# Moving one first projection in four of a dense expert layer from the expert stage into the routing-map stage, and a subtraction from VectorE to GpSimd

## Chip, cores and metric

One core of one Trainium2 chip. The metric is the device time of one execution in microseconds, the median of several. The kernel is one launch of several stages, which are parted by barriers over all engines.

## What is computed

The reference is one step of a decoder layer: attention, then a retrieval layer (PEER) in which each of 1056 tokens picks 128 of 16384 experts. Only that second half matters here:

```
q = (tb @ wq) ...; s = q . keys; top-16 of 128 first keys and of 128 second keys, top-16 of their sums
e = i1 * 128 + i2                      # expert number, weight g = softmax of the scores
a = gelu(einsum('td,thkd->thk', tb, u_tab[e]))
out = einsum('thk,thkd->td', g * a, v_tab[e])
```

The kernel computes 640 of the tokens (five tiles of 128) densely: for every first key (128 of them, each with 128 experts) it takes the projections of all 640 tokens on the key's `u` rows, gelu, times a map G of weights that is zero almost everywhere, and multiplies by the key's `v` rows. The other 416 tokens are done by gathers of single expert rows. Products are made in three parts of split numbers: high by high, high by low, low by high.

## The kernel before

**Map stage** (second part of `peer_route`, lines 1488 to 2021). For each of five tiles (ND) it goes through 32 groups (NGT) of 4 tokens, 160 groups in all. For each token TensorE multiplies two one-hot matrices of 128x128 (L2013), which makes that token's map. Of each group three left one-hots come from GpSimd (L1946), three right ones from VectorE (`rows`, L1660), and the fourth pair from ScalarE (`make`, L1881 to L1888). ScalarE moves the result out of PSUM (`leave`, L1898), and SP stores it to scratch in ten transfers of 4 MB (L1643). One-hots and maps have four slots (SLOTS), so that no engine is more than four groups ahead of TensorE. VectorE does the searches of the other tiles in between, in an order written out (`between`).

**Expert stage** (`peer_experts`, lines 2032 to 2396). It has 32 turns (NQ), each of four first keys (CQ). A turn has two halves. In the **dots half** there are eight slots m (two for each key, one for each block of 320 tokens). TensorE makes 24 products of 128x320 for each slot (L2168, L2169, L2174) into one of two PSUM banks; ScalarE takes the gelu (L2226); VectorE multiplies by the map (`weigh`, L2329); ScalarE copies the high part `ph` (L2232); VectorE subtracts it for the low part `pl` (L2334). In the **out half** TensorE makes 16 sums of 12 products each (L2190: high v by high p, L2195: low v by high p, L2199: high v by low p), and VectorE adds each to the accumulator (L2343).

The rounded parts of u and v are made by ScalarE (`split_u` L2214, `split_v` L2220) and GpSimd (`low_u` L2359, `low_v` L2363). The 416 gathered rows of a partition run beside all this, 13 in a turn: GpSimd issues the gather (L2368), VectorE takes a dot product (L2297) and later the weighted sum (L2309), with two small ScalarE operations between. The tuple BESIDE says how many dots or sums go with which slot: (2, 2, 2, 1, 2, 1, 1, 0) in the dots half, then none and 15 times one. The ring of gathered rows has four places. In the dots half GpSimd goes through the slots in order: in slots 1 and 3 `low_u`, in slots V_AT = (0, 2, 4, 5) `low_v`, then the slot's gathers. In each slot every engine's order is fixed by the program; semaphores count slots. The third sum of out slot 0 waits until the `pl` of slot 6 is there, and the second until all four `low_v` are.

Of the kernel before, what the change touches and what calls it, by code (L numbers as in the profile page):

```python
# [1489 lines left out]
def peer_route(nc, io, keep):  # L1490
# [32 lines left out]
    with ExitStack() as ctx:  # L1523
# [87 lines left out]

        with nc.Block() as block:
            @block.sync
            def _(sp):
# [25 lines left out]
                def store(i):  # L1640
                    for h in range(2):
                        sp.wait_ge(g_out, NGT * i + GROUPS * (h + 1))
                        sp.dma_start(gview[2 * i + h], G[:, h].rearrange("p i t -> p (i t)")).then_inc(g_stored[h], 16)  # L1643

                load(0)
                for i in range(ND):
                    if i + 1 < LATE:
                        load(i + 1)
                    store(i)

            @block.vector
            def _(v):
# [149 lines left out]
                def turn(i):  # L1802
                    v.wait_ge(pick_turned, i + 1)
                    if i >= 2:
                        v.wait_ge(spread, NGT * (i - 1))
                    pickT = pickTs[:, i % 2]
                    turned = turned_at(i)
                    nc.vector.tensor_copy(pickT[:, 0:3], turned[:, 0:3 * P].rearrange("p (n t) -> p n t", n=3))
                    nc.vector.tensor_scalar(pickT[:, 3], turned[:, 2 * P:3 * P], -1.0, None, ALU.mult).then_inc(pick_out, 1)
                    v.wait_ge(pick_out, i + 1)  # L1810

# [7 lines left out]
                def between():  # L1819

                    spots[0] += 1
                    for n in range(made[0], rows_before(spots[0])):
                        if n % NGT == 0:
                            turn(n // NGT)
                        rows(n // NGT, n % NGT)
                    made[0] = rows_before(spots[0])
# [7 lines left out]
            def _(act):  # L1834
# [55 lines left out]

                def leave(i, g):
# [11 lines left out]
                for i in range(ND):  # L1903
                    for g in range(NGT):
                        for n in range(LATE):
# [6 lines left out]
                        if i < ND - 1 and g % COPY_EVERY == 0:  # L1912
                            copy_window(act, io, "k", PER_TILE * i + g // COPY_EVERY).then_inc(keep.win_out, 16)
                    if NGT * (i + 1) == spread_at:
# [6 lines left out]
            def _(pool):  # L1921
# [8 lines left out]

                for i in range(ND):
                    pickT = pickTs[:, i % 2]
                    pool.wait_ge(pick_out, i + 1)
                    for q in range(NGT // SLOTS):
# [7 lines left out]
                        for u in range(SLOTS):  # L1942
                            if done + u >= SLOTS:
# [12 lines left out]
            def _(pe):  # L1956
# [35 lines left out]

                pe.wait_ge(keys_in, 16)
# [8 lines left out]
                for i in range(ND):  # L2002
                    for g in range(NGT):
# [10 lines left out]
                        x.then_inc(spread, 1)  # L2014

# [10 lines left out]
DOTS = CQ * NBD  # L2026
OUTS = NBD * KC
# [4 lines left out]
def peer_experts(nc, io, keep):  # L2032


    with ExitStack() as ctx:
# [18 lines left out]
        Gt = G.rearrange("p u h (c t) -> p u h c t", c=2)  # L2054
        hrow = sb("e_hrow", [P, D])[:]
# [11 lines left out]
        uv_in = [nc.alloc_semaphore(f"e_uv_in{u}") for u in range(RING)]  # L2067
        h_in = nc.alloc_semaphore("e_h_in")
# [21 lines left out]
        V_AT = (0, 2, 4, 5)  # L2090
# [31 lines left out]
        with nc.Block() as block:  # L2122
            @block.sync
            def _(sp):
# [7 lines left out]
                def load_u(i, c):  # L2132

                    sp.wait_ge(ul_done, CQ * i + c - 1)
                    sp.dma_start(uu[:, c % 2], uview[ds(CQ * i + c, 1)].rearrange("a p k e -> (a p) k e")).then_inc(u_in[c % 2], 16)
# [11 lines left out]
                for c in (2, 3):  # L2147
                    load_u(0, c)
                with sp.Fori(0, NQ - 1) as i:
                    for load, c in ((load_v, 2), (load_u, 4), (load_v, 3), (load_g, 4), (load_u, 5), (load_v, 4), (load_v, 5),  # L2150
                                    (load_g, 6), (load_u, 6), (load_u, 7)):
                        load(i, c)
# [4 lines left out]
            def _(pe):  # L2157
# [3 lines left out]
                def dot(i, c):  # L2161
                    pe.wait_ge(uh_done, CQ * i + c + 1)
                    for b in range(NBD):
                        m = NBD * c + b
                        pe.wait_ge(p_done, DOTS * i + m + 1)
                        cols = slice(b * WD, (b + 1) * WD)
                        for k in range(KC):
                            nc.tensor.matmul(pa[:, m % 2, 0:WD], uh[:, c % 2, k], keep.hi_d[:, k, cols], start=(k == 0), stop=False)  # L2168
                            nc.tensor.matmul(pa[:, m % 2, 0:WD], uh[:, c % 2, k], keep.lo_d[:, k, cols], start=False, stop=False)  # L2169

                        if b == 0:
                            pe.wait_ge(ul_done, CQ * i + c + 1)
                        for k in range(KC):
                            x = nc.tensor.matmul(pa[:, m % 2, 0:WD], ul[:, c % 2, k], keep.hi_d[:, k, cols], start=False,  # L2174
# [28 lines left out]
                with pe.Fori(0, NQ) as i:  # L2203
                    for c in range(CQ):
                        dot(i, c)
                    out(i)

            @block.scalar
            def _(act):
# [12 lines left out]
                def gelus(i, m):  # L2222
                    n = DOTS * i + m
                    c, b = m // NBD, m % NBD
                    act.wait_ge(dotted, n + 1)
                    nc.scalar.activation(pa[:, m % 2, 0:WD], pa[:, m % 2, 0:WD], ACT.Gelu).then_inc(gelu_done, 1)  # L2226
                    if b == 1 and c < 2:
                        split_u(CQ * i + 2 + c)
# [39 lines left out]
                act.dma_start(uu[:, 0], uview[0]).then_inc(u_in[0], 16)  # L2268
                act.dma_start(uu[:, 1], uview[1]).then_inc(u_in[1], 16)
# [6 lines left out]
                for i in range(NQ):  # L2276
# [5 lines left out]
                    for n in range(OUTS):  # L2282
                        if n in (0, 2) and i + 1 < NQ:
                            split_u(CQ * (i + 1) + n // 2)
# [4 lines left out]
            def _(v):  # L2289
# [32 lines left out]
                def weigh(i, m):  # L2322
# [3 lines left out]
                    ops = share(m)  # L2326
# [3 lines left out]
                                            pa[:, m % 2, 0:WD].rearrange("p (h t) -> p h t", h=ND),  # L2330
# [308 lines left out]
```

## Time and profile before

| what | value |
|---|---|
| median of 3 runs | 3917.97 us (3907.5 to 3925.23) |
| the profiled execution | 3920.84 us, span 3919.2 us |
| TensorE busy | 3292.2 us (84%) |
| VectorE busy | 2633.8 us (67%) |
| GpSimd busy | 1600.8 us (41%) |
| ScalarE busy | 1347.6 us (34%) |
| query part of the routing stage | about 1225 to 1545 us |
| map stage | 1545 to 1898 us |
| expert stage | 1913 to 3838 us |

Busy times are unions over an engine's instructions. The records of TensorE products overlap, so the pace of products is read from the starts of two of them, not from the duration of one. An average over the span mixes stages with different limits, so each stage is read by itself.

### The profile page before, as it was taken

What the parts mean: (1) busy time and instruction counts of PE and PEld (TensorE: products, weight loads), DVE (VectorE), ACT (ScalarE), POOL (GpSimd) and SP (SyncE); (2) the same over time, 40 slices, a digit from 0 to 9 for tenths busy, and PEclk for the clock granted to TensorE, in tenths of its full rate; (3) what the DMA queues carried; (4) which work ended last, traced back from release to release, by engine and by line L of the source; (5) the groups of instructions that cost most, each with busy time, mean ns of one, the idle gap of its engine ahead of it and who ended that gap; (6) DMA issues with size and microseconds to landing.
All of it is one profiled execution on the core that took longest, in us unless ns stands there. A gap on an engine that the chain in (4) does not pass through costs nothing. (4 is left out here: it accounts for less than half of the span.)

```text
span 3919.2 us, 58752 instructions
## 1 busy us (share of the span) xinstructions
PE 3292.2 (84%) x20585; PEld 2874.9 (73%) x20585; DVE 2633.8 (67%) x5881; ACT 1347.6 (34%) x3190; POOL 1600.8 (41%) x1345
## 2 busy tenths in 40 slices
PE   6999688656587975666699999999999999999994
PEld 3778455211277964555599999999999999999993
DVE  3224676101133799999588888888888888888885
ACT  3010466100222113878433333333333333333331
POOL 1010000000121444999645555545546455455450
PEclk8999899877788987878799999999999999999997
DMA  6631783799512222664688889888888898888883
GB/s 221 240 131 65 216 227 130 309 412 411 210 61 97 65 69 69 250 244 197 265 316 339 313 316 342 315 325 334 307 329 326 313 340 314 320 326 315 312 295 132
DMA packets 280225, 991.40 MB, mean 253 GB/s; under 512 B 21781, under 2 KB 139392, under 8 KB 215721
## 3 DMA queue, kind: packets, MB, share of 16 engines
q1 hardware_dynamic: 214504, 480.69, 33.9%
q0 software_dynamic: 62784, 469.88, 31.7%
q10 hardware_dynamic: 2752, 38.75, 2.6%
q8 instruction: 70, 1.15, 0.1%
q14 instruction: 115, 0.93, 0.1%
HBM read 909.51 MB, written 146.80 MB: 270 GB/s over the span
## 5 line engine op out<-in xcount | busy, mean ns | idle before, releaser
L2168 PE MATMUL e_pa<-k_hi_d,e_uh 128*128 128x320 f32 x2048 | 618.2, 315 | 76.3 <-DVE e_act L2329 60.6
L2169 PE MATMUL e_pa<-k_lo_d,e_uh 128*128 128x320 f32 x2048 | 607.9, 311 | 0.0
L2368 POOL DMA_INDIRECT e_uv<-peer_uv,k_g_idx x416 | 399.9, 961 | 498.9 <-DVE e_pY L2309 443.4
L2297 DVE CUSTOM_DVE_ANT_0 e_uv<-e_uv,e_h 128x1024 f32<-128x1024 f32 x416 | 503.7, 1211 | 62.4 <-DMA e_uv<-peer_uv,k_g_idx 62.2
L2309 DVE SCALAR_TENSOR_TENSOR e_pY<-e_uv,e_wts,e_pY 128x1024 f32<-128x1024 f32 x412 | 526.9, 1279 | 0.0
L2168 PEld LDWEIGHTS e_pa<-k_hi_d,e_uh 128*128 128x128 f32 x2048 | 387.3, 189 | 101.6 <-DVE e_act L2329 85.7
L2363 POOL TENSOR_TENSOR e_vl<-e_v,e_vh 128x1024 fp32r<-128x1024 f32 x128 | 308.8, 2413 | 292.8 <-ACT e_vh L2220 292.2
L2247 ACT ACTIVATE e_gel<-e_dots 128x1 f32<-128x1 f32 x416 | 83.5, 201 | 957.1 <-DVE e_dots L2297 956.8
L2190 PE MATMUL e_po<-e_ph,e_vh 128*128 128x320 f32 x2048 | 387.0, 310 | 15.3 <-DVE k_OT L2343 11.0
L2169 PEld LDWEIGHTS e_pa<-k_lo_d,e_uh 128*128 128x128 f32 x2048 | 387.5, 189 | 0.0
L2199 PE MATMUL e_po<-e_pl,e_vh 128*128 128x320 f32 x2048 | 384.0, 309 | 0.4
L2195 PE MATMUL e_po<-e_ph,e_vl 128*128 128x320 f32 x2048 | 383.4, 309 | 0.0
L2013 PE MATMUL r_pG<-k_OT 128*128 128x128 f32 x1280 | 224.8, 336 | 157.4 <-issue 53.0
L2359 POOL TENSOR_TENSOR e_ul<-e_u,e_uh 128x1024 fp32r<-128x1024 f32 x128 | 309.0, 2414 | 116.2 <-ACT e_uh L2214 114.9
L2174 PE MATMUL e_pa<-k_hi_d,e_ul 128*128 128x320 f32 x2048 | 342.5, 309 | 0.0
L2190 PEld LDWEIGHTS e_po<-e_ph,e_vh 128*128 128x128 f32 x2048 | 320.4, 188 | 22.9 <-DVE k_OT L2343 17.5
L2013 PEld LDWEIGHTS r_pG<-k_OT 128*128 128x128 f32 x1280 | 199.9, 239 | 182.4 <-issue 119.0
L1946 POOL TENSOR_SCALAR k_OT<-k_iota,r_second 128x128 f32<-128x128 f32 x480 | 325.7, 698 | 8.5 <-PE r_pG L2013 4.7
L2199 PEld LDWEIGHTS e_po<-e_pl,e_vh 128*128 128x128 f32 x2048 | 321.2, 188 | 1.4 <-DVE e_pl L2334 1.4
L2195 PEld LDWEIGHTS e_po<-e_ph,e_vl 128*128 128x128 f32 x2048 | 321.3, 188 | 0.0
L2174 PEld LDWEIGHTS e_pa<-k_hi_d,e_ul 128*128 128x128 f32 x2048 | 311.6, 188 | 0.0
L2334 DVE TENSOR_TENSOR e_pl<-e_act,e_ph 128x320 fp32r<-128x320 f32 x256 | 273.7, 1069 | 17.2 <-ACT e_ph L2232 14.5
(326 smaller groups left out, 5919.7 us busy)
## 6 DMA issues: line engine op xcount, KB each, us to landing
k_kv<-kv_pages SPq DMA_DIRECT2D x128, 512.0 KB, 6.2
s_kv<-kv_state SPq DMA_DIRECT2D x32, 2048.0 KB, 17.5
e_v<-peer_uv SPq DMA_DIRECT2D x128, 512.0 KB
e_u<-peer_ut SPq DMA_DIRECT2D x126, 512.0 KB
s_g<-r_G SPq DMA_DIRECT2D x10, 4096.0 KB
k_OT<-s_g SPq DMA_DIRECT2D x64, 640.0 KB
v_win_sample<-state_v_win POOLq DMA_DIRECT2D x28, 1168.0 KB
k_win_sample<-state_k_win ACTq DMA_DIRECT2D x28, 1168.0 KB
```

Source lines behind the costliest of these rows:

```text
L1946: x = nc.gpsimd.tensor_scalar(hot2[:, u, t], keep.iota[:], second[:, u, t:t + 1], None, ALU.is_equal)
L2013: x = nc.tensor.matmul(pG[:, u, t], hot2[:, u, t], hot1[:, u, t], start=True, stop=True)
L2168: nc.tensor.matmul(pa[:, m % 2, 0:WD], uh[:, c % 2, k], keep.hi_d[:, k, cols], start=(k == 0), stop=False)
L2169: nc.tensor.matmul(pa[:, m % 2, 0:WD], uh[:, c % 2, k], keep.lo_d[:, k, cols], start=False, stop=False)
L2174: x = nc.tensor.matmul(pa[:, m % 2, 0:WD], ul[:, c % 2, k], keep.hi_d[:, k, cols], start=False, stop=(k == KC - 1))
L2190: nc.tensor.matmul(po[:, n % SUMS, 0:WD], vh[:, c, rows], ph[:, c, cols], start=(c == 0), stop=False)
L2195: nc.tensor.matmul(po[:, n % SUMS, 0:WD], vl[:, c, rows], ph[:, c, cols], start=False, stop=False)
L2199: x = nc.tensor.matmul(po[:, n % SUMS, 0:WD], vh[:, c, rows], pl[:, c, cols], start=False, stop=(c == CQ - 1))
L2297: nc.vector.tensor_tensor_reduce(uv[:, r, 0:D], uv[:, r, 0:D], h[:], 1.0, 0.0, ALU.mult, ALU.add, dots[:, r:r + 1]).then_inc(row_dotted, 1)
L2309: x = nc.vector.scalar_tensor_tensor(out=pY[:], in0=uv[:, r, D:2 * D], scalar=wts[:, r:r + 1], in1=pY[:], op0=ALU.mult, op1=ALU.add)
L2359: nc.gpsimd.tensor_tensor(ul[:, c % 2], uu[:, c % 2], uh[:, c % 2], ALU.subtract).then_inc(ul_done, 1)
L2368: nc.gpsimd.indirect_dma_start(uv[:, s % RING], None, io["peer_uv"], bass.IndirectOffsetOnAxis(ap=keep.g_idx[:, s:s + 1], axis=0),).then_i ...
```

## The change

The first projections of the first of each turn's four keys (32 keys, 64 halves of 24 products, 1536 products) are made in the map stage. There TensorE makes some 10 of them after each group from group 12 on (`made_by`). The u rows are loaded by SP, split by ScalarE and GpSimd, the result is copied out of PSUM by ScalarE and stored by SP to a new scratch `s_p`. In the expert stage slots 0 and 1 of a turn have no products: their projections are loaded from scratch, and gelu and map product work in SBUF. Three keys in place of four are loaded and split in a turn. The low part `pl` goes from VectorE to GpSimd, before the slot's gathers, and VectorE's `weigh` waits until the `pl` of two slots before is done. `low_v` goes with slots (1, 2, 4, 5), the only `low_u` of the dots half with slot 3.

```diff
 # map stage
+        def made_by(done):
+            return max(0, HALVES * PER_HALF * (done + 1 - OPENS) // (ND * NGT - OPENS))
+        def half_at(n):
+            return next(g for g in range(ND * NGT) if made_by(g) >= PER_HALF * (n + 1))
 # SP
+                def load_u(e):
+                    if e >= 2:
+                        sp.wait_ge(ul_done, e - 1)
+                    sp.dma_start(uu[:, e % 2], io["peer_ut"][CQ * e]).then_inc(u_in[e % 2], 16)
+                def store_p(e):
+                    sp.wait_ge(p_out, NBD * e + NBD)
+                    sp.dma_start(io["s_p"][e], pout[:, e % 2]).then_inc(p_stored[e % 2], 16)
...
+                store_p(EARLY - 1)
+                for u in range(2):
+                    sp.wait_ge(p_stored[u], 16 * (EARLY // 2))
 # ScalarE
+                    nc.scalar.activation(uh[:, e % 2], uu[:, e % 2], ACT.Copy).then_inc(uh_done, 1)
...
+                    nc.scalar.activation(pout[:, e % 2, b * WD:(b + 1) * WD], pa[:, n % 2, 0:WD], ACT.Copy).then_inc(p_out, 1)
 # GpSimd
+                def low_u(e):
+                    pool.wait_ge(uh_done, e + 1)
+                    nc.gpsimd.tensor_tensor(ul[:, e % 2], uu[:, e % 2], uh[:, e % 2], ALU.subtract).then_inc(ul_done, 1)
...
+                            for e in range(2, EARLY):
+                                if done + u == half_at(NBD * (e - 2) + 1) + SLOTS:
+                                    low_u(e)
 # TensorE
                         x.then_inc(spread, 1)
+                        for m in range(made_by(done - 1), made_by(done)):
+                            early_dot(m)
 # expert stage
-        V_AT = (0, 2, 4, 5)
+        V_AT = (1, 2, 4, 5)
 # SP
+                def load_early(i):
+                    sp.wait_ge(p_done, DOTS * i + NBD + 2)
+                    sp.dma_start(early, io["s_p"][ds(i + 1, 1)].rearrange("a p t -> (a p) t")).then_inc(early_in, 16)
 # TensorE
-                    for c in range(CQ):
-                        dot(i, c)
-                    out(i)
+                        for c in range(1, CQ):
+                            dot(2 * j + half, half, c)
+                        out(2 * j + half)
 # VectorE
-                    ops = share(m)
+                    own = early[:, b * WD:(b + 1) * WD] if c == 0 else pa[:, m % 2, 0:WD]
+                    if n >= 2:
+                        v.wait_ge(pl_done, n - 1)
                     v.wait_ge(g_in[c // 2], 16 * i + 16)
                     v.wait_ge(gelu_done, n + 1)
...
-                    gathers(i, ops[:1])
-                    v.wait_ge(ph_done, n + 1)
-                    nc.vector.tensor_tensor(pl[:, c, cols], act_out[:, m % 2], ph[:, c, cols], ALU.subtract).then_inc(pl_done, 1)
-                    gathers(i, ops[1:])
+                    gathers(i, share(m))
 # GpSimd
+                def low_p(i, m):
+                    n, c, b = DOTS * i + m, m // NBD, m % NBD
+                    cols = slice(b * WD, (b + 1) * WD)
+                    pool.wait_ge(ph_done, n + 1)
+                    nc.gpsimd.tensor_tensor(pl[:, c, cols], act_out[:, m % 2], ph[:, c, cols], ALU.subtract).then_inc(pl_done, 1)
...
-                        if m % NBD == 1 and m // NBD < 2:
-                            low_u(CQ * i + 2 + m // NBD)
+                        if m == 3:
+                            low_u(UQ * i + 2)
                         if m in V_AT:
                             low_v(CQ * i + V_AT.index(m))
+                        low_p(i, m)
                         gathers(i, m)
```

## Rows read from the trace of the kernel before

**Rows 1.** Busy time by stretch (stretch, length; engine busy, instructions; granted clock, DMA share, GB/s).
```profile
1371.00:1545.00 174.00, 106.91 (x546) 99.28 (x544) 168.89 (x537) 25.26 (x65) 67.55 (x34) 0.82 0.21 61
1545.00:1900.00 355.00, 225.84 (x1289) 200.93 (x1289) 326.00 (x1342) 300.55 (x799) 338.77 (x521) 0.80 0.54 212
...
1960.00:3780.00 1820.00, 1752.37 (x11731) 1720.13 (x11730) 1507.67 (x2171) 620.11 (x1526) 964.38 (x640) 1.00 0.86 323
```
**Rows 2.** Groups of the map stage, 1545 to 1900 us (busy, mean ns | idle before, releaser).
```profile
L1946 POOL TENSOR_SCALAR k_OT<-k_iota,r_second 128x128 f32<-128x128 f32 x478 | 324.5, 698 | 8.4 <-PE r_pG L2013 4.7
L2013 PE MATMUL r_pG<-k_OT 128*128 128x128 f32 x1280 | 224.8, 336 | 157.4 <-issue 53.0 <-DVE k_OT L1660 48.2 <-POOL k_OT L1946 42.1
```
**Rows 3.** Groups of the expert stage, 1960 to 3780 us, same columns.
```profile
L2168 PE MATMUL e_pa<-k_hi_d,e_uh 128*128 128x320 f32 x1937 | 581.0, 314 | 52.0 <-DVE e_act L2329 52.0
...
L2297 DVE CUSTOM_DVE_ANT_0 e_uv<-e_uv,e_h 128x1024 f32<-128x1024 f32 x399 | 483.2, 1211 | 60.7 <-DMA e_uv<-peer_uv,k_g_idx 60.5
...
L2363 POOL TENSOR_TENSOR e_vl<-e_v,e_vh 128x1024 fp32r<-128x1024 f32 x121 | 292.0, 2413 | 280.5 <-ACT e_vh L2220 279.9
...
L2334 DVE TENSOR_TENSOR e_pl<-e_act,e_ph 128x320 fp32r<-128x320 f32 x241 | 256.6, 1065 | 16.2 <-ACT e_ph L2232 13.5 <-issue 2.7
...
L2214 ACT ACTIVATE e_uh<-e_u 128x1024 fp32r<-128x1024 f32 x121 | 126.0, 1041 | 0.0
```
**Rows 4.** GpSimd's groups over the whole span: subtractions of other widths.
```profile
L1929 POOL TENSOR_TENSOR q_wl<-r_G,q_wh 128x1024 fp32r<-128x1024 f32 x32 | 85.8, 2682 | 2.6
...
L1311 POOL TENSOR_TENSOR k_lo_d<-k_OT,k_hi_d 128x640 fp32r<-128x640 f32 x8 | 12.3, 1538 | 0.0
L1310 POOL TENSOR_TENSOR k_lo_g<-k_OT,k_hi_g 128x416 fp32r<-128x416 f32 x8 | 8.5, 1066 | 49.3 <-ACT k_hi_d L1238 49.3
```
**Rows 5.** Timeline of TensorE, one turn (start, length, operation).
```profile
3024.32 0.74 PE L2190 MATMUL e_po<-e_ph,e_vh 128*128 128x320 f32 x4
...
3053.33 0.31 PE L2168 MATMUL e_pa<-k_hi_d,e_uh 128*128 128x320 f32 x1
...
3056.85 0.31 PE L2168 MATMUL e_pa<-k_hi_d,e_uh 128*128 128x320 f32 x1
...
3083.97 0.74 PE L2190 MATMUL e_po<-e_ph,e_vh 128*128 128x320 f32 x4
```
**Rows 6.** Timeline of VectorE, then of GpSimd, start of a dots half.
```profile
3053.94 1.21 DVE L2297 CUSTOM_DVE_ANT_0 e_uv<-e_uv,e_h 128x1024 f32<-128x1024 f32 x1
...
3057.57 0.49 DVE L2329 TENSOR_TENSOR e_act<-e_pa,k_OT 128x320 f32<-128x320 f32 x1 [2.41 <-ACT e_pa L2226]
...
3059.17 0.48 DVE L2334 TENSOR_TENSOR e_pl<-e_act,e_ph 128x320 fp32r<-128x320 f32 x1
3059.57 1.21 DVE L2297 CUSTOM_DVE_ANT_0 e_uv<-e_uv,e_h 128x1024 f32<-128x1024 f32 x1
...
3061.78 0.49 DVE L2329 TENSOR_TENSOR e_act<-e_pa,k_OT 128x320 f32<-128x320 f32 x1 [0.99 <-ACT e_pa L2226]
...
3063.38 2.53 DVE L2334 TENSOR_TENSOR e_pl<-e_act,e_ph 128x320 fp32r<-128x320 f32 x1
...
3059.60 2.42 POOL L2363 TENSOR_TENSOR e_vl<-e_v,e_vh 128x1024 fp32r<-128x1024 f32 x1 [4.93 <-ACT e_vh L2220]
...
3065.71 1.03 POOL L2368 DMA_INDIRECT e_uv<-peer_uv,k_g_idx  x1 [0.16 <-issue]
```
**Rows 7.** Timeline around the end of the map stage.
```profile
1893.30 1.13 PE L2013 MATMUL r_pG<-k_OT 128*128 128x128 f32 x8 [0.39 <-issue]
...
1898.56 0.33 SPq L1643 DMA_DIRECT2D s_g<-r_G  x1
...
1911.48 1.85 SPq L2130 DMA_DIRECT2D k_OT<-s_g  x2
...
1913.58 0.63 PE L2168 MATMUL e_pa<-k_hi_d,e_uh 128*128 128x320 f32 x1 [15.68 <-ACT e_uh L2214]
```
**Rows 8.** The page's DMA issues (KB each, us to landing).
```profile
k_kv<-kv_pages SPq DMA_DIRECT2D x128, 512.0 KB, 6.2
```

More of the change, by code:

```diff
@@ L1810, in turn, with keep_turned @@
                     v.wait_ge(pick_out, i + 1)
+                def keep_turned():
+                    for i in range(2, ND):
+                        v.wait_ge(pick_turned, i + 1)
+                        nc.vector.tensor_copy(kept_turned[:, i - 2], turned_at(i)[:, 0:3 * P]).then_inc(turned_kept, 1)
                 for x in range(NHC):
@@ L1904, in _ @@
                     for g in range(NGT):
+                        if i == 0 and g in (SLOTS, SLOTS + 1):
+                            split_u(g - SLOTS)
+                        for n in range(HALVES):
+                            if NGT * i + g == half_at(n) + 1:
+                                dots_away(n)
+                                if n % NBD == NBD - 1 and n // NBD + 2 < EARLY:
+                                    split_u(n // NBD + 2)
                         for n in range(LATE):
@@ L1913, in _ @@
                             copy_window(act, io, "k", PER_TILE * i + g // COPY_EVERY).then_inc(keep.win_out, 16)
+                    if i == ND - 1:
+                        for n in range(HALVES):
+                            if half_at(n) == ND * NGT - 1:
+                                dots_away(n)
                     if NGT * (i + 1) == spread_at:
@@ L2026 @@
 DOTS = CQ * NBD
+UQ = CQ - 1
 OUTS = NBD * KC
@@ L2054, in peer_experts @@
         Gt = G.rearrange("p u h (c t) -> p u h c t", c=2)
+        early = keep.rest[:, 4 * DT:5 * DT]
         hrow = sb("e_hrow", [P, D])[:]
@@ L2145, in load_v, with quad @@
                     sp.dma_start(vv[:, c % 2], row(vview, CQ * i + c)).then_inc(v_in[c % 2], 16)
[L2147 to L2152, printed above, removed]
+                def load_early(i):
+                    sp.wait_ge(p_done, DOTS * i + NBD + 2)
+                    sp.dma_start(early, io["s_p"][ds(i + 1, 1)].rearrange("a p t -> (a p) t")).then_inc(early_in, 16)
+                def quad(i, half):
+                    load_u(i, half, UQ)
+                    load_v(i, 2)
+                    load_early(i)
+                    load_v(i, 3)
+                    load_u(i, half, UQ + 1)
+                    load_g(i, 4)
+                    load_v(i, 4)
+                    load_v(i, 5)
+                    load_g(i, 6)
+                    load_u(i, half, UQ + 2)
+                sp.dma_start(early, io["s_p"][0]).then_inc(early_in, 16)
+                load_u(0, 0, 2)
+                with sp.Fori(0, NQ // 2 - 1) as j:
+                    for half in range(2):
+                        quad(2 * j + half, half)
+                quad(NQ - 2, 0)
                 for c in (2, 3):
@@ L2201, in out @@
                             x.then_inc(summed, 1)
-                with pe.Fori(0, NQ) as i:
-                    for c in range(CQ):
-                        dot(i, c)
-                    out(i)
+                with pe.Fori(0, NQ // 2) as j:
+                    for half in range(2):
+                        for c in range(1, CQ):
+                            dot(2 * j + half, half, c)
+                        out(2 * j + half)
             @block.scalar
@@ L2224, in gelus @@
                     c, b = m // NBD, m % NBD
[L2225 to L2228, printed above, removed]
+                    if c == 0:
+                        own = early[:, b * WD:(b + 1) * WD]
+                        act.wait_ge(early_in, 16 * i + 16)
+                    else:
+                        own = pa[:, m % 2, 0:WD]
+                        act.wait_ge(dotted, NBD * UQ * i + m - NBD + 1)
+                    nc.scalar.activation(own, own, ACT.Gelu).then_inc(gelu_done, 1)
+                    if m == 3:
+                        split_u(UQ * i + 2)
                     act.wait_ge(p_done, n + 3)
@@ L2394, in _ @@
                         if n in (0, 2) and i + 1 < NQ:
-                            low_u(CQ * (i + 1) + n // 2)
+                            low_u(UQ * (i + 1) + n // 2)
                         gathers(i, DOTS + n)
```

118 lines of the change are left out of this document (94 added, 24 removed).

## The prediction

> **What bounds the kernel now.** I read the page, then busy time by stretch, then the groups and the timeline of the two stages that the change touches. In the expert stage TensorE is busy for 1752 of 1820 us at full granted clock, VectorE for 1508, GpSimd for only 964 [rows 1]: TensorE sets the pace. A turn has 64 products of L2168, of which 1937 fall into 1820 us, so a turn takes 1820 / (1937/64) = 60.1 us [rows 3]. One turn in detail [rows 5]: out half 3024.32 to 3053.33, 29.0 us; dots half 3053.33 to 3083.97, 30.6 us. A slot of 24 products takes 3.52 us, 0.1466 us for one. 192 products are 28.15 us, so the out half loses 0.85 us and the dots half 2.5 us to waits.
>
> In the map stage it is GpSimd: busy for 339 of 355 us, against 326 on VectorE, 301 on ScalarE and 226 on TensorE [rows 1], which stands idle for 157 us in its group [rows 2]. GpSimd's one-hots waited for TensorE only 4.7 us. So the change takes work from where TensorE is the bound to where it has room, but each moved key also brings a GpSimd subtraction to a stage that GpSimd bounds.
>
> **Map stage: GpSimd.** Added are 32 `low_u` of 128x1024. The same subtraction takes 2.413 us in the expert stage [rows 3]: 77 us. Beside VectorE's searches the like of it took 2.68 us [rows 4]: 86 us. Lower end 61 us, if all 16 idle us of GpSimd are filled. I take 77 plus 5 for waits behind VectorE's long operations: **+82 us**, a stage of 437 us.
>
> **Map stage: the other engines.** TensorE: eight 128x128 products take 1.13 us [rows 7], 0.141 each at most, so 1280 are at most 180 us; the 1536 moved ones at 0.1466 are 225 us. Sum 405 us at full clock, below 437. The clock was 0.80 there [rows 1], at a TensorE that was busy 64% of the time and slowed down whenever it waited; at 0.93 and more the 405 still fit, below that they don't (a rival). ScalarE gets 32 splits at 1.04 us [rows 3] and 64 copies of 320 columns, priced at 0.49 (VectorE's operation on as many, [rows 6]): 33 + 31, 365 of 437 us. VectorE gets three short copies, 2 us. All this is covered by GpSimd's 437 us; if GpSimd had more room, TensorE's 405 would be next. SP gets 32 loads and 32 stores between the ten map stores. A 4 MB store took 1898.56 to 1911.48, 12.9 us [rows 7], and a u load queued behind it waits as long; the program gives each load about five groups, 5 x 2.7 = 13 us. Cost taken as nothing; upper end in the rival.
>
> **Between the stages.** Now TensorE starts 15.0 us after the last map store is issued [rows 7]: the first u rows of the expert stage queue behind it. In the changed kernel SP must see the last `store_p` land before the barrier, and that store stands behind the map store: 12.9 us, then some 1.3 us of barrier, then a 512 KB load, whose nearest row is 6.2 us [rows 8], and a split of 1.04: 21.5 us. **+6.5 us** (0 to 10).
>
> **Expert stage: what TensorE saves.** 48 products in a turn, 48 x 0.1466 = 7.0 us, or 225 us in 32 turns, if TensorE keeps the pace. VectorE loses 241 subtractions of 257 us in this stretch, 8.5 us a turn [rows 3]; of its 49.8 (1508 / 30.3 turns) 41.3 us are left, with 2 us a turn of waits for gathered rows (60.5 us in L2297), so it bounds nothing. The question is GpSimd.
>
> **The price of the moved subtraction.** 416 columns took 1.066 us and 640 took 1.538 [rows 4], 2.11 ns per column, so 320 take **0.864 us** (bounds: 0.75 by proportion to 2.413 us for 1024, and 1.07). By the Trainium skill (GPSIMD Engine Reference, Elementwise, and Engine selection: use VectorE, GpSimd is about 2x slower with two inputs, some 2.6 cycles of 1.2 GHz per element) it would be an estimated 0.69 us with no fixed part; the chain below would be 1.0 us shorter and the forecast 33 us lower.
>
> **A turn walked through.** Let t = 0 at 3053.33, when TensorE starts the dots. VectorE's last dot product of the turn before starts at 3053.94 [rows 6]. From such a start to the next `weigh` it is 3061.78 - 3059.57 = 2.21 us (dot, two small ScalarE operations, gelu), so with its gelu input already there, `weigh` of slot 0 comes at 0.61 + 2.21 = 2.8 (now 4.2). Slots with two gather operations have a pitch of 3061.78 - 3057.57 = 4.21 now; less the 0.40 of the subtraction, 3.81. So `weigh` of slots 1 and 2 comes at 6.6 and 10.4. TensorE starts with slots 2 and 3 and has used both banks at 7.0; it waits for `weigh` 2 until 10.9.
>
> GpSimd: the first `low_v` is now in slot 1, behind that slot's `weigh`, `ph` and `split_v`; now it starts 3059.60 - 3057.57 = 2.03 us after the `weigh` [rows 6], so at 8.6. From there GpSimd never gets free until the `pl` of slot 6, on which the third sum of the out half waits. In program order: four `low_v` and one `low_u`, 5 x 2.41 = 12.1; the `pl` of slots 1 to 6, 6 x 0.864 = 5.2; the gathers of slots 1 to 4, each 0.15 + 1.03 [rows 6], 4.7; gaps 0.3. Sum 22.3, end at **30.9**. TensorE meanwhile: slot 4 from 10.9 to 14.4, slot 5 from the end of `weigh` 3 (10.4 + 3.8 + 0.5 = 14.7) to 18.2, slot 6 to 21.8, slot 7, which needs `weigh` 5 and by the new wait `pl` 3 (done at 21.0), to 25.3. It then makes 8 of the 192 out products and stands until 30.9; 184 are left: 184 x 0.1466 = 27.0, plus the 0.85 us that the out half loses today: the turn ends at **58.75**. Against 60.1 that is 1.4 us, **-44 us** in 32 turns instead of the 225. Bounds: with the `pl` at 0.75, 22 us more gain; with TensorE's pace reached, the rival below; with the first `low_v` or the v loads late by a microsecond or two, no gain, 0 us.
>
> What is queued behind GpSimd's new waits: its gathers. The gather of slot 4 goes out at about 25.6, where the ring needs the row some 9 us later; nothing more is lost there. The DMA moves 323 GB/s at a share of 0.86 [rows 1]; a turn loads a u of 0.52 MB less and 0.33 MB of projections more, so with 58.75 us it stays at about 327 GB/s.
>
> **Sum.** 3920.8 + 82 + 6.5 - 44 = 3965 for this execution, which lay 2.9 us over the median of the runs: **3962 us**, 1.1% slower. A measurement of this kernel tells a change of about 0.5% (20 us) from none.
>
> **Rivals.**
> - **TensorE keeps the pace of the expert stage** (faster). If the GpSimd chain ends before TensorE wants it, a turn is 336 x 0.1466 = 49.3 plus today's 3.4 of waits, 52.7: -237. With +88 outside it gives 3769. For it: GpSimd's work (7 x 2.41, 13 gathers at 1.03, 8 x 0.864) is 37 us in a turn of 52.7; VectorE loses its only operation that is held behind GpSimd (2.53 us against 0.48, [rows 6]). Against: of that work 22 us stand in one string that can't start before slot 1. Chance 0.12.
> - **The gain and the cost meet.** GpSimd's string ends some 2 us earlier (slots' `weigh` earlier, a cheaper `pl`), a turn of 56.5 to 57.5: -83 to -115. With +75 to +88 outside this gives 3875 to 3925, about 3905. Chance 0.23.
> - **The map stage stalls** (slower still). TensorE's 405 us at the clock of 0.80 would be 506 us; or u loads wait behind the ten map stores for 5 us each, and ScalarE with them. It decides once the granted clock stays under 405/437 = 0.93. The stage is then 460 to 505 us: 3985 to 4030. For it: the clock was 0.82 in the stretch before too, with TensorE busy 61% [rows 1]. Against: a TensorE that lags is busy all the time, and wherever it is, as in the expert stage, the clock is 1.00. By the Trainium skill (GPSIMD Engine Reference, Specifications) GpSimd shares its SBUF interfaces with VectorE's instructions that have two SBUF inputs; the 2.53 us row agrees, and this would add to this case. Chance 0.15.
> - **The forecast's own case**, 3930 to 3985, has 0.50.
>
> **Range and chances.** The range leaves out the first rival (0.12) and the outer part of the stalls: 3880 to 4015. Faster by over 0.5% (below 3898): the first rival and half of the second, 0.24. Within 0.5%: the rest of the second and the edge of the forecast, 0.17. Slower: 0.59.
>
> **What the profile would show.** Right: a map stage of 430 to 445 us with GpSimd busy throughout and TensorE idle in short pieces; in the expert stage a turn of 58 to 59 us, TensorE below 90% busy, L2199 waiting for GpSimd's `pl` by some 4 us a turn and L2168 for `weigh`; the GpSimd subtraction of 320 columns at 0.86 us. Wrong: a turn near 53 us; GpSimd idle in the dots half after slot 1; a map stage near 355 us, which would mean that GpSimd had room; or ScalarE waiting for u loads.

## The result, and the profile after

The changed kernel takes 4065.7 us (median of 4), the kernel before 3921.3 in the same runs: 1.036 times as long (95% interval 1.034 to 1.039). The forecast was 3962. Busy time by stretch of the changed kernel, columns as in [rows 1]; the map stage first, then the inside of the expert stage:

```profile
1547.00:2073.00 526.00, 402.35 (x2817) 394.32 (x2818) 364.22 (x1345) 355.94 (x893) 403.02 (x552) 0.88 0.53 192
...
2140.00:3920.00 1780.00, 1598.29 (x10255) 1569.45 (x10254) 1279.14 (x1925) 601.31 (x1494) 1081.94 (x849) 0.95 0.89 326
```

The map stage is 171 us longer than before (355 in [rows 1]), and in it no engine is busy for more than 403 of 526 us. That is what a stage looks like whose engines wait in turn for something outside them. Its groups:

```profile
L2036 POOL TENSOR_SCALAR k_OT<-k_iota,r_second 128x128 f32<-128x128 f32 x477 | 313.7, 676 | 2.9
L2127 PE MATMUL r_pG<-k_OT 128*128 128x128 f32 x1280 | 185.9, 292 | 151.9 <-issue 106.4 <-POOL k_OT L2036 34.1 <-DVE k_OT L1708 11.4
...
L2014 POOL TENSOR_TENSOR q_wl<-r_u,q_wh 128x1024 fp32r<-128x1024 f32 x32 | 78.3, 2448 | 113.8 <-ACT q_wh L1952 113.4
...
L1952 ACT ACTIVATE q_wh<-r_u 128x1024 fp32r<-128x1024 f32 x32 | 33.6, 1050 | 106.7 <-DMA r_u<-peer_ut 106.7
```

L1952 is `split_u` of the map stage: ScalarE stood still for 106.7 us until u rows were loaded, GpSimd's `low_u` (L2014) 113 us for ScalarE. Here is one of these waits, SP's issues and then ScalarE's split in the timeline:

```profile
1700.73 0.33 SPq L1668 DMA_DIRECT2D s_g<-r_G  x1
1701.10 0.43 SPq L1673 DMA_DIRECT2D r_u<-peer_ut  x1
1701.58 0.92 SPq L1677 DMA_DIRECT2D s_p<-r_pout  x1
1702.54 1.24 SPq L1648 DMA_DIRECT2D k_OT<-s_s  x1
1703.83 1.26 SPq L1673 DMA_DIRECT2D r_u<-peer_ut  x1
...
1721.06 1.06 ACT L1952 ACTIVATE q_wh<-r_u 128x1024 fp32r<-128x1024 f32 x1 [16.27 <-DMA r_u<-peer_ut]
```

The 4 MB map store goes out first, the u load 0.4 us behind it, and its rows are there 20 us later; ScalarE has waited 16.3 us, so it wanted them 3.7 us after they were asked for. While it waits it neither takes maps out of PSUM nor makes its one-hots, and with four slots all engines stop. Nine such waits fall in the stage, about one for each map store. Over the nine, ScalarE wanted the rows 3.7 to 13.9 us after the issue of the load (9 on average), and they landed 13.7 to 25.5 us after it (21 on average).

The store itself is longer than the one in [rows 7]. By the packet records of the trace its last packet ends 18.7 us after its issue, not 12.9. The DMA queues of these microseconds (1700.8 to 1719.4; packets, MB, share of the 16 engines) show what runs beside it: q1 is SP's queue, q10 ScalarE's, on which a copy of 1168 KB (`k_win_sample`) is under way:

```profile
q1 hardware_dynamic: 392, 5.29, 77.8%
q10 hardware_dynamic: 39, 1.20, 17.6%
```

It was so in the kernel before too: eight of its ten map stores take 17.7 to 24.6 us, with 1.2 MB or more moved on ScalarE's queue meanwhile, and only the last two, with 0 and 0.4 MB, take 10.8 and 12.3. [rows 7] shows the last of all. The ninth store of the changed kernel has nothing beside it, and the load behind it lands 13.7 us after its issue:

```profile
2024.96 0.33 SPq L1668 DMA_DIRECT2D s_g<-r_G  x1
2025.34 0.43 SPq L1673 DMA_DIRECT2D r_u<-peer_ut  x1
...
2039.09 1.06 ACT L1952 ACTIVATE q_wh<-r_u 128x1024 fp32r<-128x1024 f32 x1 [5.38 <-DMA r_u<-peer_ut]
```

No run took the copies away, so that they are what slows the stores is likely, but not shown.

In the expert stage TensorE starts 21.0 us after its last map product (16.0 before), and the stage then takes 2093.5 to 3981.5 = 1888 us against 1913.6 to 3838.2 = 1925 before: 37 us less, 59.0 us a turn in place of 60.1. Its groups, columns as in [rows 3]:

```profile
L2308 PE MATMUL e_pa<-k_hi_d,e_uh 128*128 128x320 f32 x1448 | 469.0, 336 | 120.9 <-DVE e_act L2477 120.9
...
L2339 PE MATMUL e_po<-e_pl,e_vh 128*128 128x320 f32 x1973 | 373.8, 311 | 23.4 <-POOL e_pl L2514 23.4
...
L2514 POOL TENSOR_TENSOR e_pl<-e_act,e_ph 128x320 fp32r<-128x320 f32 x240 | 209.0, 877 | 78.5 <-ACT e_ph L2378 78.0
...
L2443 DVE CUSTOM_DVE_ANT_0 e_uv<-e_uv,e_h 128x1024 f32<-128x1024 f32 x397 | 482.1, 1214 | 143.8 <-DMA e_uv<-peer_uv,k_g_idx 143.8
```

The moved subtraction takes 0.877 us on GpSimd. TensorE waits 121 us (52 before) for VectorE's `weigh` and 23 for GpSimd's `pl`. VectorE waits 144 us for gathered rows, where it was 60 [rows 3]. The time line of one turn, in which TensorE starts the dots at 3035.19:

```profile
3035.19 0.31 PE L2308 MATMUL e_pa<-k_hi_d,e_uh 128*128 128x320 f32 x1
...
3038.07 0.49 DVE L2477 TENSOR_TENSOR e_act<-k_OT 128x320 f32<-128x320 f32 x1 [1.06 <-ACT k_OT L2372]
...
3041.95 0.49 DVE L2477 TENSOR_TENSOR e_act<-k_OT 128x320 f32<-128x320 f32 x1 [1.06 <-ACT k_OT L2372]
...
3045.79 0.49 DVE L2477 TENSOR_TENSOR e_act<-e_pa,k_OT 128x320 f32<-128x320 f32 x1 [1.02 <-ACT e_pa L2372]
...
3043.98 2.35 POOL L2508 TENSOR_TENSOR e_vl<-e_v,e_vh 128x1024 fp32r<-128x1024 f32 x1 [2.85 <-ACT e_vh L2361]
...
3062.06 0.74 PE L2330 MATMUL e_po<-e_ph,e_vh 128*128 128x320 f32 x4
3063.82 0.86 PE L2335 MATMUL e_po<-e_ph,e_vl 128*128 128x320 f32 x4 [1.02 <-POOL e_vl L2508]
3065.45 0.85 PE L2339 MATMUL e_po<-e_pl,e_vh 128*128 128x320 f32 x4 [0.78 <-POOL e_pl L2514]
```

`weigh` of slots 0, 1 and 2 starts at t = 2.9, 6.8 and 10.6 (forecast 2.8, 6.6, 10.4), the first `low_v` at 8.8 (8.6), the third sum of the out half at 30.3 (30.9). This turn is no exception: in 29 of the 32 turns the third sum starts at 30.2 to 30.4.

One thing in this turn stands in no step of the forecast. TensorE stood still for 4 us until `weigh` of slot 2 was done, and soon after its restart the products of slot 4 follow each other at 0.267 us instead of 0.147. The granted clock of 3047 to 3050 us is 0.50, the lower of its two levels (1.2 and 2.4 GHz); the first two lines have columns as in [rows 1]:

```profile
3035.20:3042.20 7.00, 7.00 (x50) 6.92 (x48) 4.81 (x9) 2.19 (x7) 2.76 (x3) 1.00 0.81 263
3047.00:3050.00 3.00, 3.00 (x13) 3.00 (x12) 1.98 (x4) 2.06 (x5) 2.83 (x3) 0.50 0.74 177
...
3046.34 0.41 PE L2308 MATMUL e_pa<-k_hi_d,e_uh 128*128 128x320 f32 x1 [3.96 <-DVE e_act L2477]
...
3047.63 0.47 PE L2308 MATMUL e_pa<-k_hi_d,e_uh 128*128 128x320 f32 x1
3047.90 0.47 PE L2309 MATMUL e_pa<-k_lo_d,e_uh 128*128 128x320 f32 x1
...
3051.50 0.31 PE L2308 MATMUL e_pa<-k_hi_d,e_uh 128*128 128x320 f32 x1
```

Slot 4 takes 5.16 us instead of 3.52. Counted from the starts of all products of the stage, such slow products cost 77 us (19 before), and TensorE's waits 228 us (97 before). That is the whole account: 225 us of products less, 131 us of waits and 58 us of slow products more, 36 us left.

### The profile page after: what moved, and what is told of

Its sections match the earlier page's. It is cut to its first block and busy times, and to the rows that moved or that the text cites. A ratio compares the mean times of both kernels' runs of the same rounds, so it can differ in the third digit from the quotient of the medians.

```text
span 4066.2 us, 58913 instructions
## 1 busy us (share of the span) xinstructions
PE 3312.5 (81%) x20585; PEld 2911.5 (72%) x20585; DVE 2431.0 (60%) x5628; ACT 1385.3 (34%) x3254; POOL 1788.0 (44%) x1601
## 5 line engine op out<-in xcount | busy, mean ns | idle before, releaser
L2308 PE MATMUL e_pa<-k_hi_d,e_uh 128*128 128x320 f32 x1536 | 499.6, 337 | 157.8 <-DVE e_act L2477 138.7
L2309 PE MATMUL e_pa<-k_lo_d,e_uh 128*128 128x320 f32 x1536 | 494.4, 333 | 0.0
L2308 PEld LDWEIGHTS e_pa<-k_hi_d,e_uh 128*128 128x128 f32 x1536 | 321.1, 209 | 166.5 <-DVE e_act L2477 147.1
L2309 PEld LDWEIGHTS e_pa<-k_lo_d,e_uh 128*128 128x128 f32 x1536 | 322.3, 210 | 0.0
L2127 PE MATMUL r_pG<-k_OT 128*128 128x128 f32 x1280 | 185.9, 292 | 151.9 <-issue 106.4
L2488 DVE TENSOR_TENSOR k_OT<-e_po,k_OT 128x320 f32<-128x320 f32 x496 | 243.0, 490 | 107.8 <-PE e_po L2339 80.9
L2127 PEld LDWEIGHTS r_pG<-k_OT 128*128 128x128 f32 x1280 | 173.4, 206 | 159.7 <-issue 141.1
L2314 PE MATMUL e_pa<-k_hi_d,e_ul 128*128 128x320 f32 x1536 | 266.5, 317 | 0.0
L2504 POOL TENSOR_TENSOR e_ul<-e_u,e_uh 128x1024 fp32r<-128x1024 f32 x96 | 232.0, 2417 | 75.1 <-ACT e_uh L2355 74.4
L1708 DVE TENSOR_SCALAR k_OT<-k_iota,r_pickT 128x128 f32<-128x128 f32 x480 | 173.0, 422 | 151.6 <-PE r_pG L2127 150.1
```

Source lines behind the costliest of these rows:

```text
L2127: x = nc.tensor.matmul(pG[:, u, t], hot2[:, u, t], hot1[:, u, t], start=True, stop=True)
L2308: nc.tensor.matmul(pa[:, m % 2, 0:WD], uh[:, u, k], keep.hi_d[:, k, cols], start=(k == 0), stop=False)
L2309: nc.tensor.matmul(pa[:, m % 2, 0:WD], uh[:, u, k], keep.lo_d[:, k, cols], start=False, stop=False)
L2314: x = nc.tensor.matmul(pa[:, m % 2, 0:WD], ul[:, u, k], keep.hi_d[:, k, cols], start=False, stop=(k == KC - 1))
```

## The experiments

The map stage is given below from the first to the last start of a one-hot product (before 352 us, changed 525), the expert stage from TensorE's start to SP's first issue of the stage behind it (before 1925, changed 1888). Theory A, formed on the trace: the excess of the map stage is waits behind the map stores, and in the expert stage GpSimd's string sets the turn. Theory B: TensorE has no room for the moved products at the clock it is granted. Theory C: without the low part on GpSimd the turn would be longer still.

**Four u buffers.**

```diff
-        uu = nc.alloc_sbuf_tensor_at("r_u", [P, 2, KC, P], F32, offset=keep.g_at)[:]
+        UB = 4
+        uu = [nc.alloc_sbuf_tensor_at(f"r_u{n}", [P, 2, KC, P], F32, offset=at)[:]
+              for n, at in enumerate((keep.g_at, keep.g_at + 4 * KC * GTK + 4 * 2 * DT))]
...
-                    if e >= 2:
-                        sp.wait_ge(ul_done, e - 1)
+                    if e >= UB:
+                        sp.wait_ge(ul_done, e - UB + 1)
...
-                            if e + 2 < EARLY:
-                                load_u(e + 2)
+                            if e + UB < EARLY:
+                                load_u(e + UB)
```

> The changed kernel with four u buffers in the map stage in place of two, so that a u load is issued four keys ahead. Theory A (u loads queued behind the 4 MB map stores hold ScalarE, 107 us of waits in the profile): these waits go, the map stage falls from 526 to about 420 to 437 us, the time from 4066 to about 3965. Theory B (TensorE, at the clock it is granted, has no room for the moved products): the waits of ScalarE turn into waits for TensorE, the stage stays above 490 us and the time above 4030.

Measured 4024.3 us (ratio 1.027, 1.025 to 1.029), the map stage 487 us. Neither number is that of A or B. The waits of the map stage, who waited for whom:

```profile
DVE k_OT L1710 <- PE r_pG L2129: 101.0, 50, 15.6
ACT r_pout L1961 <- DMA s_p<-r_pout: 79.9, 8, 15.4
POOL q_wl L2016 <- ACT q_wh L1954: 64.9, 10, 13.8
```

No wait for u loads is left; in its place ScalarE waits 80 us for stores of the projections: it may not fill a place of `pout` again before the store from it has landed. The same obstacle, met by the next transfer in line.

**The low part back on VectorE**, all else as changed.

```diff
-                    if n >= 2:
-                        v.wait_ge(pl_done, n - 1)
+                    ops = share(m)
...
-                    gathers(i, share(m))
+                    gathers(i, ops[:1])
+                    v.wait_ge(ph_done, n + 1)
+                    nc.vector.tensor_tensor(pl[:, c, cols], act_out[:, m % 2], ph[:, c, cols], ALU.subtract).then_inc(pl_done, 1)
+                    gathers(i, ops[1:])
...
-                        low_p(i, m)                     # on GpSimd
```

> The changed kernel with the low part of the weighted gelu back on VectorE, all else as changed. Theory A (in the expert stage GpSimd's string of subtractions and gathers from slot 1 to slot 6 sets the turn of 59.0 us): the turn falls to 56.5 to 57.5 us, 50 to 80 us less, about 4000. Theory C (the low part on GpSimd is what makes the new turn as short as it is, VectorE being late otherwise): the turn grows to 60 us or more, 4100 or more.

Measured 4034.4 (1.030, 1.028 to 1.032), 31 us less than the changed kernel; the map stage is as it was (526 us), the expert stage 1857 us, 58.0 a turn. Theory C falls; of A the sign holds, and the gain is 1.0 us a turn where 1.5 to 2.5 were expected. TensorE's waits for `pl` are gone (20 us in 1500), but those for `weigh` grow from 105 to 124: VectorE is the next bound close by. VectorE's waits for gathered rows fall from 117 to 56 us in 1500, since the gathers no longer stand behind `pl` in GpSimd's order. How much of the 1.0 us is owed to the string and how much to the later gathers is not shown.

**The low part on GpSimd alone**, in the kernel before (the opposite of the diff above, and nothing else).

> The kernel before with the low part on GpSimd and VectorE's wait for it, and nothing of the early projections. If GpSimd's string sets the dots half (four low_v, two low_u, 8 low parts at 0.88 us, gathers: about 27 us from the first low_v at 4.6 us of the turn): the out half starts at 31 to 32 us in place of 30.6, a turn of 60 to 61 us, the time 3920 to 3950. If VectorE's relief counts for more: a turn of 58 us and 3850.

Measured 3949.2 (1.007, 1.005 to 1.009); 61.2 us a turn. The subtraction on GpSimd, with the wait that it brings, costs 1.0 to 1.1 us a turn in either kernel. The paths differ: here 14 of the 35 us by which the expert stage grows are more waits of TensorE and 20 are slow products, in the changed kernel 26 and 5 of 31.

**Both.**

> Both: four u buffers in the map stage and the low part back on VectorE. Theory A: the two gains add up, 100 and 50 to 80 us, about 3900, a little faster than the kernel before. Theory B: about 3980.

Measured 3999.1 (1.020, 1.019 to 1.022), 25 us less than with four buffers alone: the two gains, 41 and 31 us, add up to 67, the first being 60 us short of the expectation for the reason given above.

**Projections stored from ScalarE's queue**, each right after its copy, with four u buffers.

```diff
-                            if e:
-                                store_p(e - 1)          # on SP
...
+                        for e in range(EARLY):
+                            if NGT * i + g == half_at(NBD * e + 1) + 1:
+                                store_p(e)              # on ScalarE, behind leave(i, g)
```

> The changed kernel with four u buffers and with the projections stored from ScalarE's queue instead of SP's, so that neither u loads nor projections stand behind the 4 MB map stores. With four u buffers alone ScalarE waited 80 us for stores of projections that stood in SP's queue. Theory A (the excess of the map stage over my forecast is waits behind the map stores in SP's queue and nothing else): those 80 us go too, the map stage is 415 to 440 us instead of 487, and the time 4024 - 55 to 75 = 3950 to 3970. Theory B (TensorE's share sets the stage once the waits are gone): the stage stays above 460 us, the time above 3995.

Measured 3959.5 (1.010, 1.008 to 1.012); the map stage 427 us. GpSimd's biggest group and the two that wait for transfers:

```profile
L2039 POOL TENSOR_SCALAR k_OT<-k_iota,r_second 128x128 f32<-128x128 f32 x480 | 326.6, 698 | 3.0
...
L1945 ACT ACTIVATE q_wh<-r_u 128x1024 fp32r<-128x1024 f32 x32 | 33.5, 1047 | 1.1 <-DMA r_u<-peer_ut 1.1
...
L1952 ACT ACTIVATE r_pout<-q_pS 128x320 f32<-128x320 f32 x64 | 26.9, 421 | 9.8 <-DMA s_p<-r_pout 7.9 <-PE q_pS L2105 1.6
```

With 9 us of waits for transfers left, the stage is the forecast's 82 us (here 75) longer than before, and GpSimd is busy for 414 of 435 us:

```profile
1545.00:1980.00 435.00, 387.66 (x2825) 378.54 (x2825) 381.39 (x1361) 357.12 (x900) 414.07 (x556) 0.97 0.61 231
```

Theory A holds, B falls: TensorE has 388 us of work and is granted 0.97 of its clock once it no longer stops (0.88 in the changed kernel).

**The same with the low part on VectorE.**

> The same with the low part of the weighted gelu on VectorE. It took 25 and 31 us off in the two pairs so far (4024 to 3999, 4066 to 4034): theory A 3920 to 3940, level with the kernel before; theory B 3970.

Measured 3935.8 (1.0038, 1.0023 to 1.0052). The early projections by themselves, without the queue's waits and without the moved subtraction, leave the time about where it was: 75 us paid in the map stage, 5 between the stages, 69 gained in the expert stage (1855 us). The two profiled executions differ by 20 us; the other 9 lie before the map stage and behind the expert stage. Of the 225 us of products 69 are gained here, 106 go into more waits of TensorE and 50 into slow products.

**GpSimd's subtraction cut short in the map stage** (the low parts of the u rows of these keys are left out).

> As the first, but in the map stage GpSimd's 32 subtractions of 1024 columns are cut to 8 columns: the low parts of the u rows of these keys are left out. If GpSimd sets the map stage (my forecast), it falls by 60 to 78 us against the first, to 355 to 375 us. If TensorE sets it, by less than 20 us.

One run, without a repeat, 3934.6; the map stage 399 us, 27 less. Neither expectation came true, it lies between them: GpSimd set the stage, but TensorE, busy for 381 us, stands right behind, as the forecast had it ("if GpSimd had more room, TensorE's 405 would be next"). Without the subtraction the gain is a third of its 78 us, and even that is not GpSimd's alone: the same edit ended delays of VectorE's one-hots (last section).

**Fewer gathered-row operations in the first slots.** In each of these only the tuple BESIDE is changed.

> The last one with gathered-row operations moved from the first three slots of the dots half (where TensorE has two slots of products but VectorE four slots of work) to later ones: 0, 1, 1, 2, 2, 2, 1, 1 and one for each out slot. If VectorE's work before the product of slot 2 holds TensorE at the start of the dots half, weigh 2 comes 4 to 6 us earlier and the turn falls from 58 to 54 to 56 us: 65 to 130 us less, about 3830. If the gathers or GpSimd set the turn: no change, or slower because the gathers now bunch in the late slots.

Measured 4005.8 (1.022, 1.021 to 1.024), 70 us slower than its parent. The expectation was wrong. TensorE's waits for `weigh` fell only from 125 to 87 us in 1500 us, and those for the accumulator rose:

```profile
PE e_pa L2311 <- DVE e_act L2479: 87.3, 30, 3.2
PE e_po L2333 <- DVE k_OT L2493: 78.6, 92, 2.2
```

In the parent the second row was 5.7 us. The out half has 1.76 us for an addition and a row operation (about 1.6); one more in it makes every sum late. (The 183 us in the next expectation counted the two records of that wait, weight load and product, together.)

> The version with four u buffers, projections stored from ScalarE's queue and the low part on VectorE, and the same 11 gathered-row operations spread over the dots half as 1, 1, 2, 2, 2, 1, 1, 1 in place of 2, 2, 2, 1, 2, 1, 1, 0; the out half is left as it was. Moving one of them to out slot 0 made that half wait (183 us more of waits for the accumulator); without that the turn of 58.0 us should fall. Theory (VectorE's work before weigh 2 holds TensorE, 4.8 us a turn): weigh 2 comes 3 us earlier, a turn of 55 us, about 3840. Rival (the gathered rows arrive late when their sums bunch): 3936 or slower.

Measured 3948.2 (1.008, 1.006 to 1.010).

> The same with 1, 2, 1, 2, 2, 1, 1, 1: between the two. By the theory a turn of about 56 us, 3870; if the first of the pair is slower than 3936, this lies between.

Measured 3922.1 (1.0006, 0.9992 to 1.0020).

> Control: the kernel before, with 1, 1, 2, 2, 2, 1, 1, 1 alone. There TensorE has products in slots 0 and 1, so an early weigh 2 gains little: at most the 1.1 us that slot 4 waits, 3890 to 3920. If it gains as much as the version with early projections, the gain is the spread's, not the change's.

Measured 3991.3 (1.019, 1.017 to 1.021): the control gets slower, so the small gain of the version before this one (3936 to 3922) is the spread and the early projections together.

> The first of these four with the low part on GpSimd. By the theory of GpSimd's string it starts at the product of slot 1 (then about 2 us earlier) and lasts 22 us, so the turn is 59.0 less 2 = 57 us, 3900; VectorE's relief gives nothing more. If GpSimd's string is not the bound, it is as fast as the one with the low part on VectorE or faster.

Measured 3971.0 (1.015, 1.012 to 1.018). Of the expected gains (3840, 3870, 3890 to 3920 and 3900) none came; the first run fell to its rival, 3936 or slower. In the first and second TensorE waits 112 and 105 us for `weigh`, hardly less than 125, and 43 and 40 us for the accumulator where it was 6, and VectorE waits 104 and 96 us for gathered rows where it was 55. My reading is that the ring of four rows takes back what a shorter first slot gains; no run changed the ring, so that is argued. With this ring I found no spread that gives the 3 us a turn. The walk had priced the row operations and left out that their order sets when the next rows are asked for. What the second one does gain in the expert stage, 12 us, lies in the clock and not in the waits: the slow products cost 51 us instead of 69, the waits 209 instead of 203. The granted clock of 2200 to 3700 us is 0.98 there, 0.95 in its parent.

**Moment, queue or packet size.** The version with ScalarE's queue had changed two things, the moment of the store and its queue. First the moment alone, on SP's queue:

```diff
-                            if e:
-                                store_p(e - 1)
+                            if e < EARLY - 1:
+                                store_p(e)
```

> Four u buffers, projections stored from SP's queue, but each as soon as it is there instead of one key later. If the late issue made ScalarE wait (80 us for these stores with four buffers alone): the waits go and the time falls from 4024 to about 3960, as with ScalarE's queue. If the place in SP's queue did: it stays above 4000.

Measured 3990.2 (1.019, 1.017 to 1.021), between the two expectations, the map stage 448 us: of the 61 us between 487 and 427 the moment gives 40, the queue 21. ScalarE still waits 35.5 us for these stores.

Next the 4 MB store as eight transfers, whose packets have 4 KB instead of 32:

```diff
-                    sp.dma_start(gview[2 * i + h], G[:, h].rearrange("p i t -> p (i t)")).then_inc(g_stored[h], 16)
+                    for c in range(CUTS):
+                        js = slice(c * NK // CUTS, (c + 1) * NK // CUTS)
+                        sp.dma_start(gview[2 * i + h][:, c * (NK // CUTS) * HALF:(c + 1) * (NK // CUTS) * HALF],
+                                     G[:, h, js].rearrange("p i t -> p (i t)")).then_inc(g_stored[h], 16)
```

> The version with projections stored from ScalarE's queue (3959), each map store cut into eight transfers with packets of 4 KB instead of 32. If the DMA engines take one packet from each queue in turn, the last projections no longer land together with the last map store: TensorE starts the expert stage 15 to 18 us after the map stage in place of 21, the time 3950 to 3956. If an engine works off one queue first, no change.

Measured 3979.5 (1.015, 1.012 to 1.017). TensorE starts 19.0 us after its last map product instead of 21.0, a hint in the expected sense; but the map stage is 448 us instead of 427, with 26 us of waits for u loads where it was 1. SP takes some 7 us to issue the eight transfers, and the u load behind them goes out that much later; that this is the reason is likely and was not tested. As a whole it loses.

> The changed kernel (two u buffers, everything on SP's queue), with packets of 4 KB alone. If the order in SP's queue holds the u loads, the same bytes stand before them: 4066, no change, 107 us of waits for u loads. If the large packets do it: 3980 to 4020.

Measured 4061.5 (1.036, 1.034 to 1.038), 111 us of waits for u loads: the same as the changed kernel (107). With two buffers the size of the store's packets does not matter to these loads, which fits the view that the bytes before them do. Whether they would come sooner from another queue was not tried.

> The fastest version so far (3922: four buffers, ScalarE's queue, low part on VectorE, slots 1, 2, 1, 2, 2, 1, 1, 1) with packets of 4 KB: 3 to 8 us less, 3914 to 3919, level with the kernel before; if the packets change nothing, 3922.

Measured 3934.5 (1.0043, 1.0028 to 1.0058), above both expected values, with a map stage of 443 us instead of 431; small packets are no help here either. No version beats the kernel before. The fastest is level with it: 3922.1.

## Why the prediction was wrong

The side was right, the size was not: 3962 was forecast and 4066 measured, above the range's 4015. By its own steps:

- **Map stage, GpSimd, +82 us**: right for what it priced. `low_u` takes 2.448 us, 78 us in all; with the transfers' waits gone the stage is 75 us longer than before.
- **Map stage, SP, "Cost taken as nothing"**: this step failed. The program gives a u load about five groups, 13 us, and I had the row of a map store, 12.9 us, next to it [rows 7]. I took the two as just fitting. Neither held. SP issues in the order of the program, so the load goes out only behind the store, and ScalarE then wanted its rows after 9 us on average, not 13. And they were there after 21 us on average, not 12.9: the load's packets come behind the store's, and the store of [rows 7] was the last one, with hardly a transfer beside it, while eight of ten took 17.7 us and more in the very trace that I had. The 32 stores of projections in the same queue I counted, but gave them no price; with four u buffers ScalarE waited 80 us for them. Cost of the step: 525 - 427 = 98 us. The third rival named the mechanism, but with 5 us for each of ten; it was about 12 for each of nine (106.7). At that it would have given 3962 + 107 = 4069.
- **TensorE's clock** as the point of decision of that rival: wrong. The clock was 0.88, but as a result of the waits; without them it is 0.97. Where the clock did cost time was the expert stage, for which the forecast had 1.00 throughout: 58 us more of slow products than before.
- **Between the stages, +6.5**: measured +5.0. From the last store of projections to the first issue of the expert stage it is 11.6 us, where the sum had 12.9 + 1.3 (the 1.3 for the barrier stands in no row); load and split took 7.1 us, as priced.
- **Expert stage, -44**: measured -37, and in part by luck. The price of the moved subtraction was 0.864, measured 0.877; 0.69, the estimate by the Trainium skill (GPSIMD Engine Reference, Elementwise), leaves out a fixed part that this trace has. The walk hit the start of each `weigh` and of the first `low_v` within 0.2 us. Its end, GpSimd's string at 30.9 us, was measured at 30.3. But slot 7 ended at 26.9 us and not at 25.3, since slot 4 was made at the lower clock; the number did not suffer, because TensorE had to stand until 30.3 anyway. And "nothing more is lost there", said of the gathers behind `pl`, was wrong: VectorE's waits for gathered rows went from 60 to 144 us.
- **"GpSimd's string instead of TensorE's pace"**: half of it. Taking the `pl` off GpSimd again gains 31 us, not more, since VectorE's row operations before `weigh` of slot 2 are the next bound (TensorE waits there 4 to 5 us a turn). The 225 us that 1536 products are worth at TensorE's pace were not within reach of any order of work tried here; with the subtraction left on VectorE and the old spread 69 us of them are.

Where the rest of those 225 us goes is known: 106 us more of waits, most of them for `weigh`, and 50 us of slow products behind such waits. What it would take to get them back is not: no run had a longer ring.

## What to carry to other kernels

When work is moved under a stage that has room on its main engine, look first at what that work must fetch and store, and in which queue: a load placed behind a large store gets its turn only after the store, and two buffers cover that only if their lead, counted from the issue, is longer than both together. Take the price of such a store from one that has the same transfers beside it, not from one that runs alone. If every engine of a stage is well below full, look for a wait for a transfer, and for what is refilled only when a store has landed. Price a saving on the bound engine by walking one turn with each engine's order, since here it was 37 us instead of 225. Where TensorE stands still in such a walk, look at the granted clock of the products behind the stand: here they cost 50 to 58 us that no step had priced.

## What the runs showed of the hardware

- A small transfer on a queue of its own can still land only with a large one that is under way on another (320 and 4096 KB here). In the version with ScalarE's queue the last map store and the last projections go out 1.5 us apart, and the next stage, which needs the projections alone, starts when both are down, 11.6 us later:

```profile
1977.91 0.34 SPq L1670 DMA_DIRECT2D s_g<-r_G  x1
...
1979.37 0.34 ACTq L1956 DMA_DIRECT2D s_p<-r_pout  x1
1990.95 0.82 SPq L2248 DMA_DIRECT2D e_v<-peer_uv  x2
```

  That the DMA engines take packets of the two queues in turn, whatever their size, would explain it and the 2 us that 4 KB packets gained there; it is not shown.
- A 4 MB store took 10.8 to 12.3 us with 0.4 MB or less of another queue's transfers beside it, and 17.7 to 24.6 us with 1.2 MB or more (ten stores of the kernel before).
- The granted clock followed the stalls: in the map stage 0.88 in the changed kernel, 0.92 with four u buffers, 0.97 once the transfers no longer held it; in the expert stage 1.00 before and 0.95 in the changed kernel, where products behind a stand of 4 us were made at 0.50.
- Some of VectorE's one-hots of the map stage stand still beside a subtraction of GpSimd. Least, median and greatest duration (ns) of the same operation with the subtraction in full and cut short (the two versions with ScalarE's queue):

```profile
L1701 DVE TENSOR_SCALAR k_OT<-k_iota,r_pickT x480: 315/343/2562, 1548.2 to 1969.2; 128x128 f32<-128x128 f32 x160
...
L1701 DVE TENSOR_SCALAR k_OT<-k_iota,r_pickT x480: 316/343/527, 1546.7 to 1939.7; 128x128 f32<-128x128 f32 x160
```

  The median is the same, so it is not that all get slower: a few last as long as a whole subtraction (2.4 us). The mean is 444 instead of 361 ns, 480 x 0.083 = 40 us that I had not counted. VectorE's room covered most of it; TensorE's waits for these one-hots were 18 us with it and 8 without.
